# Experts in rolling groups of four, with each expert's scatter behind the next expert's first up chunk

## What is computed

```python
logits = xt @ w_router + b_router              # 256 tokens, 32 experts
top_val, top_idx = lax.top_k(logits, 4)
gates = softmax(top_val)
# for each expert e, for its tokens xb:
hdn = xb @ w_up[e] + b_up[e]                   # 1024 -> 2048
gate_h = minimum(hdn[:, :1024], 7)
up_h = clip(hdn[:, 1024:], -7, 7)
act = (up_h + 1) * gate_h * sigmoid(1.702 * gate_h)
y = act @ w_down[e] + b_down[e]                # 1024 -> 1024
out[token] += y * gate
```

## Time and profile before

| | |
|---|---|
| median of 3 runs | 2349.51 us (2348.63 to 2351.63) |
| span of the profiled execution | 2345.1 us |
| between median and span | 4.4 us |
| TensorE busy | 2265.2 us, 97% of the span |
| VectorE, ScalarE, GpSimdE busy | 815.0, 499.8, 154.2 us |
| moved by DMA | 601.60 MB |

### The profile page before, as it was taken

One profiled execution on the slowest core, in us unless ns is written; L12 is line 12 of the kernel. 1 busy time (PEld: TensorE's weight loads), 2 busy tenths in 40 slices (PEclk: granted clock), 3 DMA queues, 4 the chain that ended last, 5 costly groups with the idle time before them and its releaser, 6 DMA issues.

```text
span 2345.1 us, 34269 instructions
## 1 busy us (share of the span) xinstructions
PE 2265.2 (97%) x14376; PEld 1662.3 (71%) x14376; DVE 815.0 (35%) x2072; ACT 499.8 (21%) x1180; POOL 154.2 (7%) x162
## 2 busy tenths in 40 slices
PE   7999999999999999999999999999999999999998
PEld 4777888888887788887688845666665555565556
DVE  2245554578425420005664321222222222222224
ACT  3255411100024432002443211111111111111113
POOL 1000111144301000000000000000000000000000
PEclk9999999999999999999999999999999999999999
DMA  9733223234325444344332777999999999999993
GB/s 376 276 108 108 108 72 108 72 126 162 108 84 200 182 177 148 144 150 180 131 143 109 295 288 310 426 427 425 427 427 426 427 427 426 427 426 426 427 426 124
DMA packets 44196, 601.60 MB, mean 257 GB/s; under 512 B 4704, under 2 KB 7392, under 8 KB 7808
## 3 DMA queue, kind: packets, MB, share of 16 engines
q1 hardware_dynamic: 43696, 595.40, 62.8%
q10 hardware_dynamic: 336, 3.87, 0.4%
HBM read 598.20 MB, written 1.05 MB: 256 GB/s over the span
## 4 chain that ended last, share of the span: by engine, by line
PE 82%; DMA 13%; DVE 2%; ACT 2%; issue 1%; POOL 0%; SPq 0%; POOLq 0%; PEldq 0%; DVEq 0%; ACTq 0%
PE PS L1203 14%; PE PS L957 8%; PE PS L1227 8%; DMA RG<-in_w_up 7%; PE PS L702 7%; PE PS L737 6%; PE PS L686 5%; PE PS L789 5%; DMA BIG<-in_w_up 4%; PE PS L650 3%; PE PS L535 3%; PE PS L775 2%; PE PS L1239 2%; PE PS L1132 2%; PE PS L474 2%; PE PS L1331 1%
## 5 line engine op out<-in xcount | busy, mean ns | idle before, releaser
L2560 DVE TENSOR_SCALAR STAT<-PS 128x128 f32<-128x128 f32 (+1 forms) x128 | 37.9, 296 | 668.4 <-PE PS L1203 668.4
L1203 PE MATMUL PS<-BIG,XS 128*64 128x256 f32 (+1 forms) x2016 | 236.3, 384 | 6.1 <-DMA BIG<-in_w_up 6.1
L1203 PEld LDWEIGHTS PS<-BIG,XS 128*64 128x64 f32 (+1 forms) x2016 | 145.2, 138 | 95.1 <-issue 17.9
L1203 PE MATMUL PS<-RG,XS 128*64 128x256 f32 (+1 forms) x1520 | 178.0, 384 | 12.2 <-DMA RG<-in_w_up 10.2
L957 PE MATMUL PS<-XS,RG 128*128 128x256 f32 x768 | 172.1, 382 | 5.0 <-DVE XS L1997 4.1
L1382 ACT ACTIVATE BIG<-PS 128x256 f32<-128x256 f32 (+2 forms) x197 | 82.2, 432 | 441.9 <-PE PS L702 138.9
L1203 PEld LDWEIGHTS PS<-RG,XS 128*64 128x64 f32 (+1 forms) x1520 | 107.9, 137 | 80.4 <-DMA RG<-in_w_up 15.8
L957 PEld LDWEIGHTS PS<-XS,RG 128*128 128x128 f32 x768 | 145.5, 191 | 26.9 <-issue 6.9
L1846 ACT ACTIVATE STAT<-STAT 128x128 f32<-128x128 f32 (+1 forms) x128 | 40.1, 313 | 570.2 <-DVE STAT L2560 570.2
L1963 DVE TENSOR_SCALAR HOLD<-PS 128x256 f32<-128x256 f32 x27 | 11.4, 423 | 382.0 <-PE PS L510 277.9
L686 PE MATMUL PS<-HN,RG 128*128 128x256 f32 x576 | 125.1, 379 | 1.0 <-ACT HN L1431 1.0
(11 more groups left out here) (374 smaller groups left out, 3427.9 us busy)
## 6 DMA issues: line engine op xcount, KB each, us to landing
BIG<-in_w_up SPq DMA_DIRECT2D x64, 2048.0 KB, 30.5
RG<-in_w_up SPq DMA_DIRECT2D x48, 2048.0 KB, 31.3
BIG<-in_w_down SPq DMA_DIRECT2D x32, 2048.0 KB, 32.0
RG<-in_w_ff SPq DMA_DIRECT2D x31, 2048.0 KB, 8.1
RG<-in_w_ada SPq DMA_DIRECT2D x24, 2048.0 KB, 8.3
RG<-in_w_down SPq DMA_DIRECT2D x24, 2048.0 KB, 34.5
RG<-in_w_in SPq DMA_DIRECT2D x23, 2048.0 KB, 8.2
SM<-in_w_up SPq DMA_DIRECT2D x16, 2048.0 KB, 31.3
```

What stands on the lines that cost most here:

```text
L1203: i = pe.matmul(half_of(b, h, sides), Xg[:, k, 0:cap], w[:, k, h * wd:h * wd + wd], start=False, stop=k == 7)
```

## The change

It gives the experts another layout and another order.

- **Up chunks** are cut by half the contraction (4 of 8 steps) and 1024 of the 2048 columns, where they were all 8 steps and 512 columns. Chunks 0 and 1 fill one PSUM bank, 2 and 3 another. A chunk has 8 matmuls of 64 stationary columns and 512 moving, where it had 16 of 64 and 256. Down chunks likewise are 4 steps by 1024 columns, both in one bank.
- **Gather**: SEL holds four experts' selections, 64 places each. At each expert one quarter of the width is gathered for the next four experts at once, by 4 matmuls of 128 stationary columns (tokens' features) and 256 moving; the output is upright already. XT and `upright` are gone. Three quarters are gathered ahead of expert 0, the fourth in its second chunk.
- **Activation**: two rounds per expert of 128x256, where there were four of 128x128.
- **Scatter** of expert ex comes after the first up chunk of ex + 1; that of the last expert after its down chunks, behind one copy of 128x512 into YV.
- **Biases** of the down product: 8 matmuls of 32 rows ahead of expert 0.
- **Broad experts** do what narrow ones do, plus 32 more places, whose matmuls have 32 stationary columns and 256 moving, four of them to the four quarters of the PSUM partitions. The threshold for the dense path is 96 tokens, where it was 128.

```diff
+            def gather(key, j):
+                b = take(("xg",) + key)
+                for i in range(2):
+                    for tt in range(2):
+                        m = pe.matmul(banks[b][:, 256 * i:256 * i + 256], HTM[:, tt, 256 * j + 128 * i:256 * j + 128 * i + 128],
+                                      SEL[:, tt, :], start=tt == 0, stop=tt == 1)
...
+            def lower_biases():
+                for j in range(2):
+                    for q in range(4):
+                        rows = slice(32 * q, 32 * q + 32)
+                        pe.matmul(accap(2 * q + j), BD[rows, 128 * j:128 * j + 128], GTT[rows, :], start=j == 0, stop=False,
...
+            def upper_biases(ex):
+                for s in range(2):
+                    b = take(("up", ex, s), quiet=True)
+                    for h in range(2):
+                        q = 2 * s + h
+                        rows = slice(32 * q, 32 * q + 32)
+                        pe.matmul(banks[b][64 * h:64 * h + 64, :], ID2[rows, 32 * q + ex:32 * q + ex + 1].broadcast_to([32, 64]),
+                                  BUPR[rows, :], start=True, stop=False)
...
+            def scatter(ex):
+                read_out(("sc", ex))
+                read_out(("dn", ex))
+                for j in range(4):
+                    for h in range(2):
+                        rows = slice(64 * h, 64 * h + 64)
+                        m = pe.matmul(accap(4 * h + j), YV[rows, 128 * j:128 * j + 128], SCT[rows, :], start=False,
...
+            def more_picked(ex, b):
+                pe.wait_ge(s_free[b], F.n[b])
+                pe.wait_ge(s_selg, ex + 1)
                 for tt in range(2):
+                    for q in range(4):
+                        m = pe.matmul(banks[b][32 * q:32 * q + 32, 0:256], SEL2[:, tt, :], HTM[:, tt, 256 * q:256 * q + 256],
+                                      start=tt == 0, stop=tt == 1)
...
+            def more_up(b, c, w):
+                xg = XG2.rearrange("p (k s) -> p k s", k=8)
+                for kk in range(4):
+                    for q in range(4):
+                        part = w[:, kk, 512 * (q // 2):512 * (q // 2) + 512].rearrange("p (g n) -> p g n", g=2)
+                        m = pe.matmul(banks[b][32 * q:32 * q + 32, 256 * (c // 2):256 * (c // 2) + 256], xg[:, 4 * (c % 2) + kk, :],
+                                      part[:, :, 128 * (q % 2):128 * (q % 2) + 128], start=False, stop=c == 3 and kk == 3,
...
+                upper_biases(ex)
+                ahead_of = (F.turn + 1) if ex == 0 else F.turn
+                b2, b3 = F.pool[ahead_of % 4], F.pool[(ahead_of + 1) % 4]
                 if broad:
+                    more_picked(ex, b2)
+                if ex:
+                    read_out(("xg", ex - 1))
...
+                if broad:
+                    more_upright(ex, b2)
+                    more_biases(ex, b3)
                 for c in range(4):
...
+                    if ex == 0 and c == 1:
+                        gather(("first", 3), 3)
+                        read_out(("xg", "first", 2))
+                    for kk in range(4):
...
+                        for h in range(2):
+                            i = pe.matmul(banks[b][64 * h:64 * h + 64, :], XG[:, 4 * (c % 2) + kk, 64 * r:64 * r + 64],
+                                          w[:, kk, 512 * h:512 * h + 512], start=False, stop=c % 2 == 1 and kk == 3)
...
+                    if broad:
+                        if c == 0:
+                            pe.wait_ge(s_mcopy, 7 * ex + 2)
+                        i = more_up(b3, c, w)
                     i.then_inc(s_used, 1)
+                    if ex and c == 0:
+                        scatter(ex - 1)
+                pe.wait_ge(s_av, 2 * ex + 1)
+                activated(take(("at", ex, 0)), 0)
+                if broad:
+                    pe.wait_ge(s_mcopy, 7 * ex + 3)
                 if ex + 1 < NEXP:
+                    pe.wait_ge(s_sel, 2 + min(ex, NEXP - 5))
+                    gather((ex,), ex % 4)
+                b = take(("at", ex, 1))
+                pe.wait_ge(s_av, 2 * ex + 2)
+                activated(b, 1)
...
+                read_out(("at", ex, 0))
+                if broad:
+                    more_turned(ex, b2)
+                    pe.wait_ge(s_mcopy, 7 * ex + 6)
...
+            for j in range(3):
+                gather(("first", j), j)
...
+            lower_biases()
...
+                b, n, m = F.at["dn", ex]
+                act.wait_ge(s_used, 6 * ex + 6)
+                act.activation(YV, banks[b][:, :], ACT.Copy).then_inc(s_free[b], 1)
...
-            dve.tensor_scalar(FLAG[0:1, 32:33], SV[0:1, 410:411], 128.0, None, ALU.is_gt).then_inc(s_flag, 1)
+            dve.tensor_scalar(FLAG[0:1, 32:33], SV[0:1, 410:411], 96.0, None, ALU.is_gt).then_inc(s_flag, 1)
```

More of the change, by code:

```diff
@@ L1142, in gather @@
[L1142 to L1167, removed]
+                return ring(s).rearrange("p (k n) -> p k n", k=4)
+            def gather(key, j):
[4 more added lines that the diff above has]
+                                      SEL[:, tt, :], start=tt == 0, stop=tt == 1)
+                m.then_inc(s_full[b], 1)
@@ L1169, in expert, with more_scatter @@
+            def more_scatter(ex):
+                pe.wait_ge(s_mcopy, 7 * ex + 7)
+                for j in range(2):
+                    for q in range(4):
+                        rows = slice(32 * q, 32 * q + 32)
+                        pe.matmul(accap(2 * q + j), YV2[rows, 128 * j:128 * j + 128], TS2[rows, 256:512], start=False, stop=False,
+                                  skip_group_check=True)
             def expert(ex, broad):
-                Xg = XG[ex % 2]
-                cap = 128 if broad else 64
@@ L1172, in expert @@
-                sides = 1 if broad else 2
-                wd = 512 if broad else 256
+                r = ex % 4
                 if ex + 1 < NEXP:
@@ L1224, in expert @@
                         read_out(("at", ex, 1))
-                    for k in range(8):
-                        for h in range(sides):
-                            m = pe.matmul(half_of(b, h, sides), T_[:, k, :], w[:, k, h * wd:h * wd + wd], start=k == 0, stop=k == 7)
-                    m.then_inc(s_used, 1)
[L1229 to L1238, removed]
-                        m = pe.matmul(accap(d), lh, SCT[rows, :], start=ex == 0 and d % 2 == 0, stop=ex == NEXP - 1,
-                                      skip_group_check=True)
@@ L1241, in expert @@
-                m.then_inc(s_scat, 1)
+                    for kk in range(4):
+                        i = 256 * c + 128 * (kk % 2) + 64 * (kk // 2)
+                        for h in range(2):
+                            m = pe.matmul(banks[b][64 * h:64 * h + 64, :], AVT[:, i:i + 64], w[:, kk, 512 * h:512 * h + 512],
+                                          start=c + kk == 0, stop=c == 1 and kk == 3)
+                    if broad:
+                        read_out(("at", ex, 1))
+                        m = more_down(b4, c, w)
@@ L1243, in dense_take @@
+                    m.then_inc(s_used, 1)
+                if broad:
+                    more_scatter(ex)
             def dense_take(key, quiet=False):
@@ L1863, in dense @@
                     act.activation(SG[:, f % 2, :], GH[:, f % 2, :], ACT.Sigmoid, scale=1.702).then_inc(s_dsg, 1)
-            gathered(0)
+            for j in range(3):
+                gathered(("first", j), j)
             act.wait_ge(s_flag, 1)
@@ new lines, in expert @@
+                for s in range(2):
+                    b, n, m = F.at["up", ex, s]
+                    gh, sg, uh = G1_[:, s, :], S1_[:, s, :], U1_[:, s, :]
+                    dve.wait_ge(s_used, 6 * ex + 2 * s + 2)
+                    dve.tensor_scalar(gh, banks[b][:, 0:256], 7.0, None, ALU.min).then_inc(s_gh, 1 if broad or s == 0 else 2)
+                    dve.tensor_scalar(uh, banks[b][:, 256:512], 7.0, -7.0, ALU.min, ALU.max).then_inc(s_free[b], 1)
+                    dve.wait_ge(s_gh, 3 * ex + s + 1)
@@ L2570, in expert @@
+                for s in range(2):
+                    b = full(("at", ex, s))
+                    dve.tensor_copy(AVT[:, 256 * s:256 * s + 256], banks[b][:, 0:256]).then_inc(s_free[b], 1)
                 b = full(("sc", ex))
                 dve.tensor_copy(SCT, banks[b][:, 0:256]).then_inc(s_free[b], 1)
+                if broad:
+                    dve.wait_ge(s_more, 3 * ex + 3)
+                    dve.tensor_copy(TS2, banks[b2][:, :]).then_inc(s_mcopy, 1)
+                    dve.wait_ge(s_used, 6 * ex + 6)
+                    dve.tensor_copy(YV2, banks[F.at["at", ex, 1][0]][:, 0:256]).then_inc(s_mcopy, 1)
```

260 lines of the change are left out of this document (130 added, 130 removed).

## The result

The changed kernel takes 2332.42 us (median of 4 runs, 2329.73 to 2333.64), the kernel before beside it 2349.07 (2346.01 to 2351.63): ratio 0.9929 [0.9915, 0.9943], 0.7% faster. The direction was forecast; the size wasn't: 2342.5 was the forecast, 2336 the low end of its range.

The account below looks back on a forecast made before the run. The weight stream was taken to bound the experts' stage. Idle time 10.2 us less, start 2.7 later, end 0.6 longer: net -6.9 on the span of 2345.1, 2338.2; plus 4.4 to the median, 2342.5 us stated, range 2336 to 2353.

Parts of the forecast that it names:

- A chunk therefore costs 476.12 / 96 = 4.96 us: Experts' weight stream: each 2.097 MB chunk takes 4.96 us, taken from two waits before and kept after the change.
- the second line of the account: Stretch from the issue of chunk 21 to the wait for chunk 189: forecast 1.5 us shorter.
- The stall on return: TensorE coming back from the broad expert's code: 2.0 us of stall, taken from the trace of before, held in release 1433.3.
- the walk: Chunk-by-chunk reckoning of releases in experts 0 and 1: first release at 1358.1 us, stream idle 16.2 us for 26.4.
- -6.0: Issue of chunk 21, at the end of expert 1: forecast 6.0 us earlier than 1444.7 us before.
- 4.4 us between span and median: Added to the forecast span of 2338.2 us to give the median: 2342.6, stated as 2342.5.
- +0.6: Behind the last down chunk: the copy for the scatter now stands open, so the end takes 0.6 us longer.
- The term m: Broad expert's up and down chunks: extra work for the 32 places, taken as 2.0 us a chunk, ends 1.7 and 7.2.
- pairs only: Rival, broad expert: 32-column groups run two at a time, m (extra time per chunk) 3.7 us, 2352.9 us; chance 0.10.
- no overlap: Rival, broad expert: 32-column matmuls run in turn, m (extra time per chunk) 7.2 us, 2374 us; chance 0.03.
- TensorE the bound: Rival, narrow experts: each takes 30.8 us for 26.6, over the stream's 29.8, so 2374 us; chance 0.06.
- nothing gained: Rival, expert 1: missed VectorE waits, 8 us in all, undo the 6.9 us gain, 2350.6 us; chance 0.09.

Follow-up runs that it names:

- a pair without the broad expert: Changed kernel with expert 1 run as narrow, its last 12 tokens left out, without and with eight already-met waits behind each narrow matmul: 2319.27 and 2324.04 us.
- the steps split: Changed kernel with all but four of an expert's 24 steps cut again into matmuls of 256 moving columns, same work: 2345.83 us, ratio 0.9999.
- the eight waits: Changed kernel with eight waits on an already met semaphore behind each narrow up and down matmul: 2353.88 us, ratio 1.0031.
- without the broad expert: Kernel before the change with expert 1 run as narrow, its last 12 tokens left out: 2321.25 us, ratio 0.9888.
- the exchange: Kernel before the change with experts 1 and 16 exchanged in weights and router, same output: 2332.23 us, ratio 0.9945.
- the scatter put back: Changed kernel with each scatter again directly behind its own expert's down chunks: 2335.08 us, ratio 0.9956.
- its experts exchanged: Changed kernel with experts 1 and 16 exchanged in weights and router, so the broad expert comes seventeenth: 2318.82 us, ratio 0.9882.
- its biases moved as well: Changed kernel with experts 1 and 16 exchanged and the down biases moved behind expert 0's last up chunk: 2317.73 us, ratio 0.9880.

## Why the prediction was wrong, step by step

**The step that failed** is "A chunk therefore costs 476.12 / 96 = 4.96 us", carried over to the changed kernel ("4.96 us per chunk afterwards") as if it were a property of the weights' bytes. The text had even set the excess over the bytes aside ("the rest is about what instructions take") without asking whether the change alters it. It halves TensorE's matmuls per chunk, and the period fell to 4.921. From the landing of chunk 21 to that of chunk 189 it is 834.5 us before and 827.2 after: 7.2 of the 7.5 us in the second line of the account. That the number of instructions sets this part is shown by two kernels with the change's order of landings and more code (4.952 and 4.959, forecast from the theory), and by a pair without the broad expert that restart alike (4.932, 4.963); so neither the order nor the earlier restart does it.

**What the landings say of the means.** The trace also holds when each chunk landed, in sixteen parts, and when each fetch started. In every kernel a chunk mostly lands 4.894 us after the one ahead of it, and the first of its sixteen parts keeps to 4.896 us throughout. What differs is how often the last part comes late. At 4.894 us the 168 chunks above would take 822.2 us: 12.3 us are lost before, with 57 fetches, and 5.0 after, with 31. Ten landings more than 0.2 us late hold 11.5 of the 12.3, ten others 4.9 of the 5.0, and each of the twenty comes within 6.4 us of the start of a fetch. Over the 13 executions in which the stream isn't broken between 1500 and 2290 us it is 117 of 120, where 31% would by chance. So the fetches are seen at work, though no run changed them and nothing else. Most of them delay no landing. That it takes one that meets the part already behind is a reading, not shown: a chunk's first and last part drift apart from 0.9 to 12.8 us before, and from 2.0 to 6.6 after. By it, like counts of fetches can go with 4.922 (the change) and 4.932 (without its broad expert).

**The stall on return** (2.0 us in "The 1433.3 holds 2.0 us") was copied from the earlier trace rows. It isn't there after; with the steps split it is, at 1.4 us, and with the eight waits at 3.7. So it depends on the code, and was carried over like the period: 2.0 us more gained. These stalls aren't waits for nothing. Before's lasts until 1438.43, and an instruction fetch runs from 1436.02 to 1436.95; each of the nine stalls on entry to or return from the broad code, in six kernels, ends 1.3 to 2.1 us behind the end of a fetch.

**The other terms before chunk 21.** The first release came 12.3 us behind the start of the first gather where the walk had 10.7: 1.6 lost, 1.4 of it the gathers at a lower granted clock. The first gather itself began at 1344.85, 2.3 us earlier than before's (1347.11) and 2.6 earlier than the walk's 1347.4. That much needs no cause in the change: in the two variants of the kernel before above, which have the same instructions ahead of it, the first issue stands at 1360.84 (without the broad expert) and 1350.91 (with the exchange).

```profile
1360.84 3.78 SPq L2795 DMA_DIRECT2D BIG<-in_w_up  x2
```
```profile
1350.91 3.78 SPq L2795 DMA_DIRECT2D BIG<-in_w_up  x2
```

So -6.0 became -6.0 - 2.6 + 1.6 - 2.0 = -9.0, where -8.6 is read. A forecast built on one execution has that spread in it. Of the same kind is the 4.4 us between span and median. The changed kernel's profiled execution has a time of its own, 2333.22 us for the span of 2331.3, so 1.9 lie outside the span. By that, before's profiled one took 2347.0, 2.5 us under its median, and after's 0.8 over its own. These 3.3 us and the 6.9 of the span are the 10.1 by which the forecast was off.

**The end.** +0.6 was forecast, +2.4 came: 0.8 waiting for the copy, and 1.7 for a down chunk at half the clock. TensorE had waited 0.54, 1.24 and 1.64 us shortly before. In the second execution of the same kernel that chunk took 3.65 us behind the same wait of 1.64, as it did with the scatter put back, so it comes and goes.

**What held.** A chunk of a narrow expert 3.48 to 3.58 us (3.45 forecast), gather 1.73 (1.75), scatter 1.93 (1.95), a narrow expert 1457.15 - 1430.51 = 26.64 (26.6), six chunks of broad code at 5.45 (5.45), 6.3 us from the last up to the first down chunk (6.6). The term m, bounded only between 1.7 and 7.2, measured 1.87: 32 instructions of 0.21 are 6.9 us in turn, so 3.7 run at a time. That rules out the rivals of pairs only and of no overlap. The Trainium skill's 3.07 for four row tiles ("TensorE: Matmul & The Clock Gate", Part 3) would have made it 2.25 by that estimate; the four column groups here come nearer to the full four. What changing the tiling mode costs, which the Trainium skill warns of as a drain ("TensorEngine Tiling (Array Packing)", Key Properties), is small here: 1.86 for 1.71 at full overlap, and 3.58 for the 3.48 of a chunk in a row of three, at most 0.26 us for two changes (0.3 forecast).

**TensorE the bound, nothing gained**: neither. TensorE's share fell from 344.85 to 336.43 of 347 us, in a stretch where that was worth nothing in itself, as forecast. Two slips in the prediction change nothing in it: one of the fourteen slices of the earlier trace rows reads 425, not 426 or 427, and "3.2 us of errors" would only bring a narrow expert level with the stream, where the 30.8 us need 4.2.

**Where the gain is, then.** In the account of two executions: about 8.6 us before chunk 21 (2.3 of it within what like kernels differ by), 7.5 along the stream, 2.4 given back at the end. In medians: the broad expert became about 13 us cheaper, and the rest of the change isn't told from nothing, since what the shorter code wins along the stream about pays for the later restart and the open copy at the end. The two ways of reading it agree within their uncertainty; how much of the 7.5 us a median would show stays open.

## What to carry to other kernels

A stream that runs "at full bandwidth" still has a cost per chunk that depends on how much code the engines run beside it: take it from two waits far apart in the chain, not from the GB/s row, and count instructions when a change alters them. Where work with a burst of long steps (here one broad expert) meets a full ring, put it where the ring has won the most lead; that was worth more (13 us) than anything else tried on top of the change. Before a sum is set against a median, ask how far the profiled execution itself stands from its own time.

## What the runs showed of the hardware

- Instruction fetches show as a DMA queue of 16 KB packets (91 to 120 a run). More of them went with a longer weight chunk: 4.921 to 4.932 us at 91 to 95, 4.952 to 4.963 at 115 to 120. Where no landing was late, a chunk took 4.894 us in every kernel, and 117 of 120 late ones came within 6.4 us of the start of a fetch.
- TensorE can stall where it branches to or from the broad code, and the view of waits names nothing for it: 3.08, 5.05 and 6.3 us on entry, 2.03, 1.4 and 3.7 on return, none in the changed kernel, 0.9 on return with its experts exchanged, 1.2 on entry and 0.3 on return with its biases moved as well. Each ended 1.3 to 2.1 us behind the end of an instruction fetch. The granted clock behind the three long entry stalls was 0.50 to 0.61, so the next operations took up to twice as long. Here is the stretch behind the 3.08 us:

```profile
1800.00:1808.00 8.00, 6.43 (x17) 2.34 (x18) 1.83 (x4) 0.00 (x0) 0.00 (x0) 0.55 1.00 423
```

- Four groups of 32 columns with 256 moving in fp32 run 3.7 at a time: 32 instructions in 1.87 us.
